# Weight halves of the second block: ten buffers from slot 22 on instead of from slot 25 on

## What is computed

```python
h = rmsnorm(x, norm_w)
z = h @ w_in        # gla q,k,v,gate, low-rank forget input; retention q,k,v,gate
o_a, s_gla = gla(q_a, k_a, v_a, la, s_gla)   # prompt: in chunks from a zero state
o_b, s_ret = ret(q_b, k_b, v_b, s_ret)       # sample: one recurrent step from a given state
mixed = concat(norm(o_a) * silu(gate_a), norm(o_b) * silu(gate_b))
y = x + mixed @ w_out
```

## Time and profile before

| | us |
|---|---|
| median of three runs | 1668.95 |
| profiled execution, own time | 1668.71 |
| span of the profile | 1666.9 |
| PE busy | 1641.7 (98%) |
| POOL busy | 840.0 (50%) |
| ACT busy | 618.6 (37%) |
| PE on the chain that ended last | 90% of the span |

### The profile page before, as it was taken

One profiled execution on the slowest core, in us unless ns is written; L12 is line 12 of the kernel. 1 busy time (PEld: TensorE's weight loads), 2 busy tenths in 40 slices (PEclk: granted clock), 3 DMA queues, 4 the chain that ended last, 5 costly groups with the idle time before them and its releaser, 6 DMA issues.

```text
span 1666.9 us, 26235 instructions
## 1 busy us (share of the span) xinstructions
PE 1641.7 (98%) x9742; PEld 1346.4 (81%) x9742; DVE 1064.9 (64%) x2388; ACT 618.6 (37%) x1166; POOL 840.0 (50%) x645
## 2 busy tenths in 40 slices
PE   6999999999999999999999999999999999999998
PEld 4788878887788887888878888788887888878886
DVE  7743666867765575547855467767787557784474
ACT  4423444243342343423443234342333424442342
POOL 4443645645455464444544445556554555554455
PEclk9999999999999999999999999999999999999999
DMA  7634657656564474467643566567864466553554
GB/s 266 154 109 110 183 203 221 192 155 169 194 177 128 114 208 133 120 151 160 202 134 97 151 143 196 163 172 188 193 193 132 122 163 158 171 173 103 142 155 142
DMA packets 389136, 268.19 MB, mean 161 GB/s; under 512 B 290704, under 2 KB 293136, under 8 KB 389008
## 3 DMA queue, kind: packets, MB, share of 16 engines
q1 hardware_dynamic: 315136, 131.99, 31.6%
q10 hardware_dynamic: 73872, 134.51, 25.6%
HBM read 219.34 MB, written 47.07 MB: 160 GB/s over the span
## 4 chain that ended last, share of the span: by engine, by line
PE 90%; DVE 4%; DMA 2%; issue 1%; SPq 1%; POOL 0%; ACT 0%; ACTq 0%; POOLq 0%; DVEq 0%
PE bank L733 78%; PE bank L994 2%; PE bank L1000 1%; PE bank L978 1%; PE bank L956 1%; PE bank L798 1%; PE bank L935 1%; SPq L442 1%; DMA region<-in_x_prompt 1%; PE bank L700 1%; DMA out_k_rows<-region 1%; DMA w_stage<-in_w_slots 1%; PE bank L939 1%; PE bank L1011 0%; PE bank L808 0%
## 5 line engine op out<-in xcount | busy, mean ns | idle before, releaser
L274 POOL TENSOR_TENSOR w_lo<-w_stage,w_hi 128x512 fp32r<-128x512 f32 x264 | 371.7, 1428 | 331.3 <-ACT w_hi L267 331.2
L733 PE MATMUL bank<-h_hi,w_hi 128*128 128x512 f32 x1024 | 408.3, 399 | 4.1 <-DVE h_lo L357 4.1
L733 PE MATMUL bank<-h_lo,w_hi 128*128 128x512 f32 x1024 | 399.8, 390 | 0.0
L733 PE MATMUL bank<-h_hi,w_lo 128*128 128x512 f32 x1024 | 399.4, 390 | 0.0
L274 POOL TENSOR_TENSOR w_lo<-ss,w_hi 128x512 fp32r<-128x512 f32 x164 | 224.3, 1387 | 211.2 <-ACT w_hi L267 211.1
L267 ACT ACTIVATE w_hi<-w_stage 128x512 fp32r<-128x512 f32 x264 | 153.8, 624 | 369.1 <-PE bank L733 286.8
L733 PEld LDWEIGHTS bank<-h_hi,w_hi 128*128 128x128 f32 x1024 | 192.4, 188 | 55.4 <-issue 8.1
L733 PEld LDWEIGHTS bank<-h_hi,w_lo 128*128 128x128 f32 x1024 | 192.5, 188 | 41.1
L733 PEld LDWEIGHTS bank<-h_lo,w_hi 128*128 128x128 f32 x1024 | 192.7, 188 | 37.2
L733 PE MATMUL bank<-w_hi,m_hi 128*128 128x512 f32 x512 | 200.6, 392 | 2.0 <-DVE region L1592 2.0
L733 PE MATMUL bank<-w_hi,h_hi 128*128 128x512 f32 x512 | 201.1, 393 | 0.0
(11 more groups left out here) (218 smaller groups left out, 2209.9 us busy)
## 6 DMA issues: line engine op xcount, KB each, us to landing
w_stage<-in_w_slots ACTq DMA_DIRECT2D x264, 256.0 KB, 3.7
ss<-in_w_slots ACTq DMA_DIRECT2D x164, 256.0 KB, 3.6
v_b<-in_w_slots ACTq DMA_DIRECT2D x84, 256.0 KB, 3.7
region<-in_x_prompt SPq DMA_DIRECT2D x32, 512.0 KB, 5.2
out_o_rows<-region SPq DMA_DIRECT2D x64, 256.0 KB, 3.1
region<-out_o_rows SPq DMA_DIRECT2D x192, 64.0 KB, 3.4
xn<-in_x_t SPq DMA_DIRECT2D x16, 512.0 KB, 5.0
out_k_rows<-region SPq DMA_DIRECT2D x32, 256.0 KB, 3.9
```

What stands on the lines that cost most here:

```text
L274: pool.tensor_tensor(w_lo[:, r, c], stage(h), w_hi[:, r, c].bitcast(f32), ALU.subtract).then_inc(lo_done, 1)
L733: i = pe.matmul(P[q][:, :], x, y, start=(s == 0 and kk == 0 and c == 0), stop=(s == 3 and kk == 1 and c == 2), skip_group_check=True)
```

## The change

One limit: in passes of kind 1, halves 42 to 47 (slots 22 to 24) go to h % 10 instead of h % 4.

```diff
         def buffer(h):
-            return h % HALVES % STAGED if h // HALVES % NBLK == 1 and h % HALVES < 48 else h % STAGES
+            return h % HALVES % STAGED if h // HALVES % NBLK == 1 and h % HALVES < 42 else h % STAGES
```

## The result

| | median us | lowest to highest |
|---|---|---|
| before | 1668.9 | 1668.67 to 1671.54 |
| after | 1676.72 | 1676.17 to 1678.24 |

The change makes the kernel slower by 7.8 us: 1.0044 times the time before, with a 95% interval of 1.0031 to 1.0057. The profiled execution of the changed kernel is its slowest, 1678.24 us, with a span of 1676.4.

The account below looks back on a forecast made before the run. PE, busy 98% of the span, was taken to bound the kernel. The terms -2.1 (pass 1), 0 (pass 1's new wait) and +11.5 (pass 5) summed to +9.4 us, 1678.35 us on the median, range 1674.0 to 1683.5.

Parts of the forecast that it names:

- T: Pass 5, load 364: moment ACT goes on after waiting for the gla_s stores; taken as 1195.3, between 1193.7 and 1198.1.
- rival (b): Pass 5: DVE makes up its lag, only the wait at slots 20 and 21 remains; net +7.0, 1675.95 us; chance 0.07.
- A gain of 2.1 us: Pass 1: loads 112 and 113 no longer wait for POOL's splits, so PE's wait behind L1592 goes; -2.1 us.
- ACT's wait for the stores there: Pass 1, load 106: ACT waits 1.2 us for the gla_s stores, at no cost to PE.
- early by several us: Pass 1: without its 6.21 us of idleness for m_hi, DVE would be early by several us.
- Loss = T - 1183.8: Pass 5, slot 25: DVE's row to silu(1) ends last and shifts everything behind; 11.5 us, 9.9 and 14.3 at the ends.
- Forecast were 2.5: Pass 5, in front of slot 25: PE waits a second time, for DVE's silu(1), 2.5 us.
- My lower end of 1193.7: Pass 5: earliest moment ACT goes on, from pass 1's quickest store, 3.9 us, counted from 1189.8.
- Rival (a): Pass 5: the store lands as late as now, 1198.1; +12.2 us, 1681.2 us; chance 0.14.
- Rival (c): Pass 5: stores land by 1183.8, the wait costs nothing and only pass 1's 2.1 us remain; 1666.85 us; chance 0.04.
- Rival (d): Pass 5: PE's clock falls in its 7.9 us wait, costing 1.4 us, hidden under DVE; chance of a visible price 0.08.
- the small wait forecast in front of slot 21: Pass 5: PE waits for the first step of silu(0), smaller than its wait of about 8 us for L1189.

Follow-up runs that it names:

- pass 1 alone: The kernel before with the limit at 42 instead of 48 in pass 1 only, pass 5 staying at 48: 1666.31 us, 0.9981 times before.
- the kernel before with narrow splits: The kernel before with POOL's splits of halves 46 to 49 in pass 5 cut to 8 of 512 columns, result incomplete: 1668.68 us, 0.9996.
- the limit of 46: The changed kernel with the limit at 46 instead of 42 in both passes: 1670.57 us, 1.0007 times the kernel before.
- the kernel with the stores moved: The changed kernel with the gla_s stores of pass 5 issued ahead of SP's 32 activation loads: 1666.37 us, 0.9984 times before.
- With T 5 us earlier: The changed kernel with the gla_s stores of pass 5 issued ahead of the last 8 of SP's 32 loads: 1673.5 us, 1.0028 times before.
- the transpose moved: The changed kernel with DVE's turning of the next block's activations in pass 5 at w = 27 instead of 23: 1676.07 us, 1.0036 times before.

## Why the prediction was right

**The sum.** I predicted +9.4 us (1678.35, range 1674.0 to 1683.5); measured are +7.8, with an interval of 5.2 to 9.5. Both effects, their places and their signs are as forecast. That the profiled execution took 1678.24 us where 1678.1 was forecast is luck: it holds the 1.5 us of pass 3, which happen to make up for a T taken too late. And by the median alone rival (b), at 1675.95, is nearer to 1676.72 than the forecast; only the traces decide against it.

**Pass 1.** A gain of 2.1 us was forecast, and 2.1 (by the second reading 2.0) is in the trace. ACT's wait for the stores there was forecast at 1.2 us and is 1.07, and is covered as forecast. DVE was not early by several us, though: silu(1) starts at 392.09, and PE needs it by about 393.15. A step that took 0.29 us in the kernel before (L1414) took 2.42. Only 1.1 us were to spare.

**Pass 5, the formula.** Loss = T - 1183.8 gave 10.3 for the T that came, and 10.27 was measured; three traces with T from 4.3 to 14.1 us behind S agree. So the choice of DVE's row as what ends last, against rival (b), was right: with the T that came, (b) gives 7.9 us for pass 5, and PE waits 1.48 us in front of slot 25. Forecast were 2.5; most of the rest went into the slow clock, below.

**T itself** was the term that was mis-sized. I took 1195.3 on the clock of the trace of before; it was 1193.29 with the whole pass 0.79 earlier (1180.02 - 1179.23), that is 1194.08. ACT went on 4.36 us after the first store's issue (1188.93), where I took 5.5 and gave 5 to 8 as the sign to look for, and the two stores landed 3.1 and 3.8 us after their own issues. My lower end of 1193.7 was also worked out wrongly: it counts from the issue of the first store, but ACT waits for the second, issued 0.5 us later. Counted from that one it is 1194.2, and T lies just under it. I had given the two weight loads beside the stores too little weight. In the three traces in which they go out beside the stores (the kernel before, pass 1 alone, the kernel before with narrow splits) the stores of pass 5 land in 5.0 to 7.8 us; in the six in which ACT stands at load 364 for them, in 3.0 to 3.9. The weights are not all of it, since with the limit of 46, where ACT issues nothing beside the stores either, they take 3.4 to 5.3 us. T makes 1.2 of the 1.6 us between forecast and result; the trace cannot place the other 0.4, which is the size of the variation between executions.

**Rival (a)**, a late landing, is out: 3.8, not 7.8 us. **Rival (c)**, the stores before T = 1183.8, did not happen by itself, but its price and its point are what the kernel with the stores moved shows: nothing lost in pass 5, 1666.37 against the 1666.85 given for it. **Rival (d)**, the clock, came true and was hidden as worked out. The pair after the wait took 4.83 us (1195.44 to 1200.27) in place of 2.97, so 1.9 us, a little over the 1.4 taken. Of these, about 1.0 us fell into the time in which PE would have waited for silu(0), so the small wait forecast in front of slot 21 did not come. PE reached slot 25 still 1.48 us before DVE. By the rule of the Trainium skill, "TensorE: Matmul & The Clock Gate", section "What's actually happening", cited there, the trace agrees that the clock fell in the long wait; that it fell in a wait of 2.28 us too (limit of 46), and did not in one of 2.27, came from the runs only.

**What I had not seen**: that DVE's row is no constant. Here it stayed at 25.38 us, by luck. With T 5 us earlier it was 26.70, and the formula missed by 1.3; with the transpose moved it was 24.27, where 20.8 would have been left.

## What to carry to other kernels

A wait for a buffer costs what stands behind the waiting instruction on its engine, not what the buffer holds: here 256 KB that PE did not need for 20 us held up a 1.1 us copy that two engines needed at once. Before a buffer is taken back earlier, look up in every pass where the transfer that frees it stands in its queue; the same line was harmless in pass 1 and cost 10 us in pass 5, since 32 loads were ahead of the store. Moving the store ahead of them, or taking the change in pass 1 alone, keeps the gain: 0.998 times the time before. And when one engine comes late, its work meets other work of the neighbours than before, so a row of durations may not be carried over from the old trace.

## What the runs showed of the hardware

**POOL's splits hold DVE up.** A norm on DVE (L1586, 128x128, a single tensor input) takes 0.27 us alone and up to 1.41 us in the kernel before; eight take 1.65 us where POOL's splits are made narrow, and 2.68 to 5.87 where splits of 1.3 us run beside them. The products L1603, with two inputs, go from 0.68 to 1.79 us. One meeting with a pair of splits costs DVE about 2 us (3.73 - 1.65) of a row of 25. The Trainium skill, "SBUF — State Buffer", section "SBUF: two separate sides", has the rule: GpSimd and a DVE operation that runs in a two-port mode, or reads two inputs in SBUF, share a pair of ports, which the first to start holds to the end of its instruction while the other stands. The measured sizes fit this: the longest norm is the short one plus 1.14 us, less than one split. That the norm runs in such a mode, and that POOL is held up in turn, no run here tests.

**The clock can fall in a wait of 2.3 us.** After 2.28 us PE ran seven matmuls at 1.2 GHz (granted clock 0.60), after 2.27 and 1.96 us none. A wait of this size can thus cost its own length or 1.65 us more. What decides between the two, no run here shows.
